# Thirteen of sixteen experts get fewer slots, by their rank in token count, and their weights are loaded through a table

## What is computed

```
    g_sel = jnp.argmax(p_group, axis=-1)
    ...
    top_w, top_i = lax.top_k(p_e, TOP_K_IN_GROUP)
    expert_id = g_sel[:, None] * EXPERTS_PER_GROUP + top_i
    ...
    h = jax.nn.silu(jnp.einsum('nd,edf->nef', xf, w_g)) * jnp.einsum('nd,edf->nef', xf, w_u)
    out = jnp.einsum('nef,efd->nd', h * gates[..., None], w_d)
```

## Time and profile before

| | us |
|---|---|
| median of three runs | 569.36 |
| the profiled execution, its own time | 567.37 |
| its span, first to last instruction | 565.3 |
| what lies around the span (567.37 - 565.3) | 2.1 |
| start of the first expert's products | 358.62 |
| end of the last expert's products | 544.7 |

### The profile page before, as it was taken

One profiled execution on the slowest core, in us unless ns is written; L12 is line 12 of the kernel. 1 busy time (PEld: TensorE's weight loads), 2 busy tenths in 40 slices (PEclk: granted clock), 3 DMA queues, 4 the chain that ended last, 5 costly groups with the idle time before them and its releaser, 6 DMA issues.

```text
span 565.3 us, 7700 instructions
## 1 busy us (share of the span) xinstructions
PE 548.0 (97%) x3042; PEld 355.4 (63%) x3042; DVE 215.0 (38%) x544; ACT 162.1 (29%) x310; POOL 98.1 (17%) x116
## 2 busy tenths in 40 slices
PE   8899999999999999999999998999999999999994
PEld 6577755544454455565444444878888788877851
DVE  3435386422222333326333755524223232222138
ACT  7332676712122132222223154111111111111132
POOL 3016000134000000003100202332322333232100
PEclk8999999999999999999999999999999999999999
DMA  9999997899400000069510239899999999999674
GB/s 282 356 334 336 330 363 318 299 387 334 168 1 0 0 1 1 0 231 352 164 56 37 83 115 361 239 304 350 350 330 328 340 352 350 341 324 346 191 205 169
DMA packets 73640, 133.21 MB, mean 236 GB/s; under 512 B 4154, under 2 KB 49634, under 8 KB 71554
## 3 DMA queue, kind: packets, MB, share of 16 engines
q1 hardware_dynamic: 59008, 99.36, 50.9%
q0 software_dynamic: 9536, 28.75, 18.3%
q10 hardware_dynamic: 5058, 4.58, 2.4%
HBM read 117.47 MB, written 18.35 MB: 240 GB/s over the span
## 4 chain that ended last, share of the span: by engine, by line
PE 90%; DVE 5%; DMA 2%; issue 1%; ACT 1%; SPq 1%; ACTq 0%
PE psum L723 86%; PE psum L726 4%; DMA ring<-in_w_mod_dram 2%; DVE arena L2192 1%; DVE x L2197 1%; SPq L509 0%; DVE arena L2111 0%; ACT uT L1360 0%; ACT arena L1360 0%; ACTq L1600 0%; DVE uT L1774 0%; DVE gst L1982 0%; DVE arena L2055 0%; DVE arena L2067 0%; DVE rtb L2111 0%
## 5 line engine op out<-in xcount | busy, mean ns | idle before, releaser
L723 PE MATMUL psum<-ring,uT 128*128 128x512 f32 (+1 forms) x384 | 126.5, 522 | 0.0
L723 PEld LDWEIGHTS psum<-arena,ring 128*128 128x128 f32 x1024 | 116.8, 192 | 8.4 <-issue 8.4
L723 PE MATMUL psum<-arena,ring 128*128 128x128 f32 x1024 | 117.0, 275 | 1.0 <-DVE arena L2250 1.0
L1360 ACT ACTIVATE arena<-psum 128x512 f32<-128x512 f32 (+6 forms) x95 | 44.9, 495 | 230.5 <-PE psum L723 160.7
L723 PEld LDWEIGHTS psum<-ring,uT 128*128 128x128 f32 (+1 forms) x384 | 56.5, 172 | 60.1 <-issue 55.8
L723 PE MATMUL psum<-uT,ring 128*128 128x288 f32 x256 | 64.9, 410 | 1.3 <-ACT uT L1360 1.3
L723 PE MATMUL psum<-ring,arena 128*128 128x512 f32 x128 | 58.7, 602 | 0.0
L723 PEld LDWEIGHTS psum<-uT,ring 128*128 128x128 f32 x256 | 47.7, 190 | 17.5 <-issue 5.1
L1360 ACT ACT_TABLE_LOAD x33 | 42.3, 1283 | 3.1 <-issue 2.1
L2296 DVE TENSOR_TENSOR arena<-arena,psum 128x128 f32<-128x128 f32 x32 | 9.2, 288 | 86.9 <-PE psum L723 86.9
L723 PEld LDWEIGHTS psum<-ring,arena 128*128 128x128 f32 x128 | 23.0, 190 | 23.0 <-issue 23.0
(11 more groups left out here) (216 smaller groups left out, 455.3 us busy)
## 6 DMA issues: line engine op xcount, KB each, us to landing
ring<-in_w_mod_dram SPq DMA_DIRECT2D x24, 1024.0 KB, 11.7
ring<-in_w_exp_gate_dram SPq DMA_DIRECT2D x16, 1024.0 KB, 15.2
ring<-in_w_exp_up_dram SPq DMA_DIRECT2D x16, 1024.0 KB, 15.5
ring<-in_w_exp_down_dram SPq DMA_DIRECT2D x16, 1024.0 KB, 13.0
ring<-in_w_in_dram SPq DMA_DIRECT2D x10, 1024.0 KB, 10.6
ring<-in_w_out_dram SPq DMA_DIRECT2D x4, 1024.0 KB, 7.1
f_dram<-in_consts_dram POOLq DMA_DIRECT2D x1, 3072.0 KB, 19.4
arena<-in_state_ret_dram POOLq DMA_DIRECT2D x6, 512.0 KB, 5.5
```

The source lines that it names most:

```text
L723: return nc.tensor.matmul(out, lhsT, rhs, start=first, stop=last)
L1360: return nc.scalar.activation(out, src, func, **kw).then_inc(done, 1)
```

## The change

Experts 0, 1 and 2 keep their places and 128 slots (`FIXED`). The other thirteen are ranked by token count. The one of rank r (0 is the largest) gets 128 - 4r slots, and `PLACES` says in which place of the order each rank runs: 11, 0, 10, 1, 9, 2, 8, 3, 7, 4, 6, 5, 12. The slots of places 3 to 15 are thus 84, 128, 88, 124, 92, 120, 96, 116, 100, 112, 104, 108, 80. Every operation of an expert takes its number of slots as its width, except where the width is 512 columns of weights.

What the places hold is known only at run time. DVE therefore computes `perm`, a 13x13 matrix of zeros and ones (`find_places`, `find_order`), and multiplies ranks and gate weights by it (`sort_columns`), so that column e of `rankp` and `gatep` belongs to place e. SP reads the expert's number from `order` into a register and adds it to the address of its load (`load_chosen`). `over` is now set when any count is above the slots of its rank.

```
+FIXED = 3
+SORTED = NE - FIXED
+FEWER = 4
+PLACES = (11, 0, 10, 1, 9, 2, 8, 3, 7, 4, 6, 5, 12)
+SLOTS_AT = [P] * FIXED + [P - FEWER * at for at in PLACES]
...
+            def load_chosen(e):
+
+                which = sp.value_load(order[0:1, e - FIXED:e - FIXED + 1], min_val=0, max_val=NE - 1)
+                for kind, w, n in (("wg", w_exp_gate, FE), ("wu", w_exp_up, FE), ("wd", w_exp_down, D)):
+                    p = (kind, e, 0)
+                    sp.wait_ge(*used[before[p]])
+                    sp.dma_start(ring[:, slot[p], :].rearrange("p (k n) -> p k n", n=n),
+                                 w[0, bass.ds(which, 1)].rearrange("a (k p) n -> p (a k) n", p=P))\
+                        .then_inc(landed[slot[p]], 16)
...
-                for p in late:
-                    load(p)
+                sp.wait_ge(s_order, 1)
+                for e in range(FIXED, NE):
+                    load_chosen(e)
...
                 for t in range(TILES):
-                    last = mm(bank[7][:, 128:129], hit[e % 2][:, t, :], tok[:, t:t + 1],
+                    last = mm(bank[7][0:n, 128:129], hit[e % 2][:, t, 0:n], tok[:, t:t + 1],
                               t == 0, t == TILES - 1)
...
-                        last = turn(bank[2 + k // 4][:, (k % 4) * P:(k % 4 + 1) * P],
-                                    xg[e % 2][:, k * P:(k + 1) * P])
+                        last = turn(bank[2 + k // 4][:, (k % 4) * P:(k % 4) * P + n],
+                                    xg[e % 2][0:n, k * P:(k + 1) * P])
...
-                                last = mm(out, w[:, k, m * P:(m + 1) * P], xgT[e % 2][:, k, :],
+                                last = mm(out, w[:, k, m * P:(m + 1) * P], xgT[e % 2][:, k, 0:n],
...
-                            last = mm(bank[4 + c][:], hT[e % 2][:, k * P:(k + 1) * P],
+                            last = mm(bank[4 + c][0:n], hT[e % 2][:, k * P:k * P + n],
...
-            link(v.tensor_reduce(out=count1, in_=bank[7][:, TILES * NE:(TILES + 1) * NE], axis=AX.X,
-                                 op=ALU.max))
+            v.tensor_copy(tally[:], bank[7][:, TILES * NE:(TILES + 1) * NE]).then_inc(s_tl, 1)
...
+            def find_places():
+
+                big = key[:, FIXED:]
+                tt(perm[:], big[:, None, :].to_broadcast(pairs), big.unsqueeze(2).to_broadcast(pairs),
+                   ALU.is_gt)
+                link(v.tensor_reduce(out=place[:, FIXED:], in_=perm[:], axis=AX.X, op=ALU.add))
+                link(v.scalar_tensor_tensor(out=key[:], in0=place[:], scalar=float(FEWER),
+                                            in1=tally[:], op0=ALU.mult, op1=ALU.add))
+                link(v.tensor_reduce(out=count1, in_=key[:], axis=AX.X, op=ALU.max))
+
+            def find_order():
+
+                tt(perm[:], place[:, None, FIXED:].to_broadcast(pairs),
+                   con[:, C_PLACE:C_PLACE + SORTED].unsqueeze(2).to_broadcast(pairs), ALU.is_equal)
+                tt(mixed[:, 0:SORTED, :], perm[:],
+                   con[:, None, C_IOTA + FIXED:C_IOTA + NE].to_broadcast(pairs), ALU.mult)
+                link(v.tensor_reduce(out=key[:, 0:SORTED], in_=mixed[:, 0:SORTED, :], axis=AX.X,
+                                     op=ALU.add))
+                v.tensor_scalar(order[:], key[:, 0:SORTED], -1.0, None, ALU.add).then_inc(s_order, 1)
+
+            def sort_columns(nth_sort, out, src):
+
+                link(v.tensor_copy(out[:, :, 0:FIXED], src[:, :, 0:FIXED]))
+                for t in range(TILES):
+                    rows_t = slice(t * SORTED, (t + 1) * SORTED)
+                    v.tensor_tensor(out=mixed[:, rows_t, :], in0=perm[:],
+                                    in1=src[:, t, None, FIXED:].to_broadcast(pairs),
+                                    op=ALU.mult).then_inc(s_sorted, 1)
+                dve.wait_ge(s_sorted, TILES * (nth_sort + 1))
+                return v.tensor_reduce(out=out[:, :, FIXED:],
+                                       in_=mixed.rearrange("p (t r) e -> p t r e", r=SORTED),
+                                       axis=AX.X, op=ALU.add)
...
-                for e in range(1, AHEAD):
-                    hits(e)
-                    numbers(e)
-
+                hits(1)
+                find_order()
+                numbers(1)
+                hits(2)
+                link(sort_columns(0, rankp, rank1))
+                numbers(2)
+                take_input(0)
+                for h in range(2, NH):
+                    new_state(h)
                 gate_weights()
...
-                v.tensor_tensor(out=gates[:], in0=oh[0], in1=oh[1], op=ALU.add).then_inc(s_gw, 1)
-                take_input(0)
-                for h in range(2, NH):
-                    new_state(h)
+                tt(oh[0], oh[0], w16(rm1), ALU.mult)
+                tt(oh[1], oh[1], w16(rm2), ALU.mult)
+                tt(gates[:], oh[0], oh[1], ALU.add)
+                sort_columns(1, gatep, gates).then_inc(s_gw, 1)
```

More of the change, by code:

```diff
@@ L206, in build @@
         over = sb("over", [P, 1], I32)
+        order = sb("order", [P, SORTED], I32)
+        key = sb("key", [P, NE])
+        tally = sb("tally", [P, NE])
+        place = sb("place", [P, NE])
+        perm = sb("perm", [P, SORTED, SORTED])
         slot_tok = sb("slot_tok", [P, NE], U32)
@@ L668, in gather_input @@
                 pool.indirect_dma_start(
-                    out=xg[e % 2], out_offset=None, in_=u2_dram,
-                    in_offset=bass.IndirectOffsetOnAxis(ap=slot_tok[:, e:e + 1], axis=0))\
+                    out=xg[e % 2][0:n], out_offset=None, in_=u2_dram,
+                    in_offset=bass.IndirectOffsetOnAxis(ap=slot_tok[0:n, e:e + 1], axis=0))\
                     .then_inc(s_xg[e % 2], 16)
@@ L1695, in take_input @@
                         act.wait_ge(s_in, 3 * (e - 1))
-                    f(xgT[e % 2][:, 0:4, :].rearrange("p k i -> p (k i)"), bank[2][:], ACT.Copy,
-                      s_xgTa)
+                    n = SLOTS_AT[e]
+                    f(xgT[e % 2][:, 0:4, 0:n], bank[2].rearrange("p (k i) -> p k i", i=P)[:, :, 0:n],
+                      ACT.Copy, s_xgTa)
                 def take_out(e):
+                    n = SLOTS_AT[e]
                     act.wait_ge(s_down, e + 1)
@@ L1715, in _ @@
                         act.wait_ge(s_hm, FT * (e - 1))
-                    f(hb[e % 2], bank[0][:, 0:FE], ACT.Silu, s_hs)
+                    n = SLOTS_AT[e]
+                    f(hb[e % 2].rearrange("p (m i) -> p m i", i=P)[:, :, 0:n],
+                      bank[0][:, 0:FE].rearrange("p (m i) -> p m i", i=P)[:, :, 0:n], ACT.Silu, s_hs)
                     if e + 1 < NE:
@@ L2084, in _ @@
             v.memset(logit[:], 0.0).then_inc(s_tl, 1)
-            dve.wait_ge(s_tl, 3 * MT + 1)
+            v.memset(place[:], 0.0).then_inc(s_tl, 1)
+            dve.wait_ge(s_tl, 3 * MT + 2)
             dve.wait_ge(s_qkT, TILES)
@@ L2160, in hits @@
                     dve.wait_ge(s_tokn, e - 1)
-                shape = [P, TILES, P]
-                v.tensor_tensor(out=hit[e % 2],
-                                in0=con[:, None, C_IOTA:C_IOTA + P].to_broadcast(shape),
-                                in1=rank1[:, :, e:e + 1].to_broadcast(shape),
+                n = SLOTS_AT[e]
+                shape = [P, TILES, n]
+                at = rank1 if e < FIXED else rankp
+                v.tensor_tensor(out=hit[e % 2][:, :, 0:n],
+                                in0=con[:, None, C_IOTA:C_IOTA + n].to_broadcast(shape),
+                                in1=at[:, :, e:e + 1].to_broadcast(shape),
                                 op=ALU.is_equal).then_inc(s_hit, 1)
@@ L2177, in _ @@
+            dve.wait_ge(s_tl, 3 * MT + 3)
             hits(0)
+            link(v.scalar_tensor_tensor(out=key[:], in0=tally[:], scalar=float(NE),
+                                        in1=con[:, C_REV:C_REV + NE], op0=ALU.mult, op1=ALU.add))
+            find_places()
             v.tensor_scalar(over[:], count1, float(CAPACITY), None, ALU.is_gt).then_inc(s_over, 1)
```

74 lines of the change are left out of this document (45 added, 29 removed).

## The result

| | before | changed | ratio |
|---|---|---|---|
| first comparison | 568.73 | 589.67 | 1.0347 [1.0297, 1.0397] |
| run again beside the experiments | 568.46 | 589.92 | 1.0361 [1.0328, 1.0393] |

The forecast was 570.0 within 566.8 to 573.2. Of the four executions behind 589.67 one took 597.6 us, over 1.5% above the fastest, and the ratios are of the others. The profile shown as "after" is that of the second row's kernel, the changed one word for word; its execution took 593.45 us, the longest of four, with a span of 591.3. Its first expert starts at 361.70 us. In a profile of the first comparison that was 365.9, so some 4 us there were scatter of one execution.

The account below looks back on a forecast made before the run. PE was taken as the bound, by its own instruction pace. +1.5 (routing) + 0.3 (gate table) + 1.1 (f16 loads) - 2.1 (transposes) - 0.2 (first load) = +0.6, so 569.36 + 0.6 = 570.0; range 566.8 to 573.2.

Parts of the forecast that it names:

- The transposes: PE, eight per expert, bound by moving columns at 0.85 ns each: 2.1 us gained, the change's whole sure gain.
- The failed step: DMA traffic of gathers and adds: some 0.2 MB less per expert; PE waits for no weights, so nothing gained.
- The products at 7.15 us: PE, 64 f32 products per expert: bound by stationary loads, so narrower ones gain 0, at most 0.5 us in all.
- the sign that was named: Right if, in the new trace, 64 products on PE of an expert with 84 columns still take 7.15 us.
- The rival of products that shorten: PE's products shorten with their columns at 0.85 ns a column: 16.8 us gained, 553; chance 2%.
- The 16 us: PE's narrower products, estimated by the Trainium skill's gap for an isolated product: change worth some 16 us; not adopted.
- The first load of `expert_out`: PE: narrower stationary load, not hidden behind the short f16 products: 0.2 us gained (ends 0 and 0.3).
- The f16 loads: PE, `slot_tokens` with narrower `hit` for twelve experts: 1.1 us lost, between no change and 2.1 lost.
- The routing: DVE's detour ahead of the experts: `over` comes 1.2 us later, experts start at 360.1; 1.5 us lost.
- The gate table: Sorted gate weights ready at 366.7, 8.9 late, delaying the gather of expert 0's gate weights: 0.3 us lost.
- the rival built on it: Table too late: ACT and DVE wait in `take_out(0)`, PE ahead of expert 1's second half; 2.0 lost, 571.7; chance 20%.
- The rival of the falling clock: PE's longer idle time ahead of 351.77 makes the clock fall: 1.7 us of products lost, 571.7; chance 5%.

## A version from what held

Narrower transposes were the sure gain, the routing the sure cost, narrow transfers the disaster. The largest count is 114, so 116 columns do for all experts without any sorting. In the kernel before, everything that PE, DVE and ACT do for an expert gets 116 columns or rows; transfers and `hit` keep 128.

```
-CAPACITY = P
+CAPACITY = 116
+N = CAPACITY
...
-                        last = turn(bank[2 + k // 4][:, (k % 4) * P:(k % 4 + 1) * P],
-                                    xg[e % 2][:, k * P:(k + 1) * P])
+                        last = turn(bank[2 + k // 4][:, (k % 4) * P:(k % 4) * P + N],
+                                    xg[e % 2][0:N, k * P:(k + 1) * P])
```

> The kernel before with 116 columns or rows in every product, transpose and operation of the experts, and nothing else changed: all transfers keep 128 rows, the five small f16 products keep 128 columns, no sorting and no table. By theory S with the rows: the transposes get shorter by 12 columns x 128 x 0.85 ns = 1.3 us, the 32-column-block products stay bound by their weight loads at 0.11 us, nothing waits for weights: 566.5 to 568, against 568.5. If a product went by its width: 12 columns x 1024 x 0.42 ns = 5 us more off, about 562.

Measured: 566.62, 0.9976 [0.9957, 0.9995], the fastest kernel here. By the ratio it is 1.4 us faster than before. The interval just leaves out a ratio of 1, and the gain is below the 0.3% that I took as the limit. PE's timeline:

```profile
504.79 0.96 PE L727 MATMUL psum<-con,arena 116*128 116x116 f32 x8
505.59 0.27 PE L724 MATMUL psum<-tok,arena 128*128 128x1 f16 x5
505.72 3.67 PE L724 MATMUL psum<-ring,arena 128*116 128x512 f32 x8
509.22 7.30 PE L724 MATMUL psum<-arena,ring 128*128 128x116 f32 x64
```

The transposes take 505.59 - 504.79 = 0.80 instead of 0.87, the f16 group stays at 0.13 with 128 columns.

## Why the prediction was wrong, step by step

**The failed step** is one sentence at the end of the change's parts: "Narrower gathers and adds take some 0.2 MB off each expert's traffic (24 slots of 4 KB, read and added); PE waits for no weights, so nothing is gained there." It counted bytes, took the sign for granted, and had no bound on the other side. The edit to the number of rows was thus priced at 0 and was worth 589.9 - 569.7 = 20 us: PE did wait for weights, 17.9 us among the experts, and lost some 4.8 more to the clock at two of these waits. Nothing in the trace of before shows a gather or an add of other than 128 rows, so it should have had an upper end from the nearest rows. These were at hand, though they give no number of rows at which the harm begins. In the earlier trace rows the DMA share is 1.03 with 311 GB/s, so there is no bandwidth to lose. And PE "waits for no weights" said only that the loads were in time, not by how much. No rival let the weights come late; none would have given 590.

**The products at 7.15 us.** Right. 64 products start 439.95 - 432.73 = 7.22 us ahead of what follows at 124 columns and 454.28 - 447.09 = 7.19 at 92. With 84 columns, the sign that was named, it is 403.71 - 396.61 = 7.10. The rival of products that shorten is dead. The 16 us that the prediction estimated from the Trainium skill's gap for an isolated product (TensorE: Matmul & The Clock Gate, "Back-to-back issue gap") doesn't follow from N/2.4 ns alone: 312 columns x 64 products / 2.4 is 8.3 us, and 16 takes the 0.85 ns a column of the transposes. Neither came.

**The transposes.** Right. At 92 columns 440.58 - 439.95 = 0.63, that is 0.079 each; 92 x 0.85 ns is 0.078.

**The first load of `expert_out`.** Priced at 0.2 in all. Its eight instructions take 408.32 - 404.84 = 3.48 us with 84 rows and 3.51 with 128, which is too little in one expert to tell the term from nothing.

**The f16 loads.** Right in size, with luck: 1.1 was the middle between two ends, and nothing in the rows had told which. 440.80 - 440.58 = 0.22 us for the group at 96 columns instead of the 0.13 of the earlier trace rows; the narrow groups of this profile take 0.19 us (80 columns) to 0.25 (120 and 124). Some 0.09 more over twelve experts is 1.1, as predicted, and less than the 1.4 of the other estimate. The rule of the Trainium skill that only 128 weights load fast (TensorE: Matmul & The Clock Gate, "Weight-path perf modes") is borne out: 124 columns cost more than 128, which no proportional rule gives.

**The routing.** Right to a tenth. DVE's timeline of the changed kernel, which answers to the earlier trace rows:

```profile
352.15 0.34 DVE L2151 TENSOR_TENSOR perm<-key 128x169 f32<-128x169 f32 x1
...
353.30 0.15 DVE L2259 TENSOR_SCALAR over<-arena 128x1 int32<-128x1 f32 x1
...
358.07 1.32 DVE L2246 TENSOR_TENSOR arena<-perm,arena 128x169 f32<-128x169 f32 x5
359.42 1.03 DVE L2250 TENSOR_REDUCE arena<-arena 128x65 f32<-128x845 f32 x1
...
360.88 0.68 DVE L2332 COPY arena<-psum 128x512 f32<-128x512 f32 x1
...
367.27 1.03 DVE L2250 TENSOR_REDUCE arena<-arena 128x65 f32<-128x845 f32 x1
```

and PE's, which answers to the earlier trace rows:

```profile
352.18 0.27 PE L753 MATMUL psum<-tok,arena 128*128 128x1 f16 x5
354.61 1.96 PE L753 MATMUL psum<-arena 128*128 128x512 f32 x4 [2.16 <-issue]
```

This execution was 1.6 us late before the routing began: the first `slot_tokens` starts at 352.18 instead of 350.60. Measured from there, `take_input(0)` starts 8.70 later, where 359.3 - 350.6 = 8.7 was predicted, and the first expert 9.52 later, against 358.62 - 350.60 = 8.02 before: +1.50, as predicted. PE's wait ahead of the branch grew to 2.16 (predicted 2.1) and the clock didn't fall there. The kernel with all slots 128 agrees with the sum, +1.7 with an interval of 0.4 to 3.0.

**The gate table.** The sorted table is ready at 368.3, predicted 366.7 with the same 1.6 of shift. ACT and DVE did wait for the first gather of it (7.1 and 6.6 us), and PE did not: its groups in the chain follow each other without idle time, 11.7 us apart (369.96, 381.68). The 0.3 can't be told from nothing, and the rival built on it didn't occur. The rival of the falling clock came true in another place, at the waits for weights. (The trace of before has a second fall besides that of the earlier trace rows, in its last 2.2 us, where it costs nothing.)

**The sum.** Without its narrow transfers the changed kernel is 1.1 us over before (569.74, interval 0 to 2.2), and +0.6 was predicted. So every term that can be read stood, within 1 us, but the one that was never priced.

## What to carry to other kernels

The number of rows in a gather or scatter is the number that decides over how many DMA engines it is spread. Round it up to a multiple of 16 and let compute be as narrow as it likes; the two widths need not be the same. Where the DMA engines are busy throughout, fewer bytes are no sign of less time: look at the largest share that one engine gets, and at how much earlier than needed the weights land. The share alone is not enough, as 120 rows show; a multiple of 16 cost at most 0.3% by the ratio in every run here. An edit whose kind of transfer no row of the trace shows has no price of zero, and it needs an upper end as a rival even if its bytes fall.

## What the runs showed of the hardware that I had not expected

The spread itself: 124, 116 and 92 rows go over 4 engines, 120 over 15, 121 over 11. With the gathers of inputs at 120 rows the engines stay as busy (1.07 against 1.06) and move 303 instead of 339 GB/s, and the kernel loses 15.5 us, though no engine has more rows; gathers of 64-byte rows and adds with 120 rows lose nothing that the runs can tell (ratios 1.0011 and 1.0007). The engines left out carry 4 or 8 bytes for each row of the others. SP's issue of a 1 MB load is no fixed cost: between 0.4 and 10.1 us before the change, up to 13.0 after it. And an idle PE costs twice: after 9.7 us without work the next 77 instructions took 10.2 instead of 8.2 us at a mean clock of 0.78.
